# A decoder layer on one core: the sparse tile's output rows, queries and choice go first and on raw weights, and 64 dense tokens instead of 32 take their down products from gathered rows

## The reference

```python
x = x + concat(short_conv(h), hgrn2(h)) @ w_out     # h = rmsnorm(x)
x = x + memory_cross_attention(rmsnorm(x), rmsnorm(mem), wq, wkv, wo)
h = rmsnorm(x)
q = h @ w_query                                     # 8 heads x 2 halves x 128
s = einsum('nhpd,hpkd->nhpk', q, sub_keys)          # 128 keys a half
s_top, i_top = top_k(s, 16)                         # then 16 of the 256 sums: expert_idx, gate
a = gelu(einsum('nd,nhkd->nhk', h, expert_down[expert_idx]))
y = einsum('nhk,nhkd->nd', gate * a, expert_up[expert_idx])
out = rmsnorm(x + y, final_norm_w)
```

## Time and profile before

| | |
|---|---|
| median of 3 runs | 1629.14 us (1626.0 to 1629.47) |
| the profiled execution | 1624.01 us |
| its span, first to last instruction | 1622.3 us |
| granted TensorE clock | 0.999 |
| busy: PE, PEld, DVE, ACT, POOL | 1600.3, 1422.6, 1133.7, 673.2, 829.1 us |
| moved by DMA | 424.69 MB, mean 262 GB/s |

### The profile page before, as it was taken

One profiled execution on the slowest core, in us unless ns is written; L12 is line 12 of the kernel. 1 busy time (PEld: TensorE's weight loads), 2 busy tenths in 40 slices (PEclk: granted clock), 3 DMA queues, 4 the chain that ended last, 5 costly groups with the idle time before them and its releaser, 6 DMA issues.

```text
span 1622.3 us, 26556 instructions
## 1 busy us (share of the span) xinstructions
PE 1600.3 (99%) x9227; PEld 1422.6 (88%) x9227; DVE 1133.7 (70%) x2214; ACT 673.2 (41%) x998; POOL 829.1 (51%) x523
## 2 busy tenths in 40 slices
PE   8999999999999999999999999999999999999998
PEld 6888888788889999999999999998888888888886
DVE  4155451351509999996999898329888888888887
ACT  5342453451534343534545544444333333333333
POOL 4463276423244998987787777866422222222220
PEclk9999999999999999999999999999999999999999
DMA  4322242313434999997999999949999999999992
GB/s 184 93 100 71 75 151 94 104 53 117 146 102 131 347 340 332 329 335 233 339 405 394 387 403 401 362 158 391 400 348 350 331 349 339 349 334 348 339 331 77
DMA packets 154425, 424.69 MB, mean 262 GB/s; under 512 B 15728, under 2 KB 65904, under 8 KB 154224
## 3 DMA queue, kind: packets, MB, share of 16 engines
q1 hardware_dynamic: 89088, 229.41, 40.5%
q0 software_dynamic: 41472, 151.01, 25.5%
q10 hardware_dynamic: 23792, 43.33, 6.9%
HBM read 379.88 MB, written 43.25 MB: 261 GB/s over the span
## 4 chain that ended last, share of the span: by engine, by line
PE 69%; issue 16%; POOL 9%; DVE 2%; DMA 2%; ACT 1%; POOLq 0%; SPq 0%; ACTq 0%; DVEq 0%
PE psum L1471 22%; PE psum L1473 22%; PE psum L1472 22%; POOL w_low L461 8%; PE psum L1766 4%; DMA gate_dram<-arena 1%; DMA kept<-down_in 1%; POOL arena L493 1%; DMA arena<-down_rows,arena 0%; DVE arena L1258 0%; ACT w_high L581 0%; DVE arena L1202 0%; DVE arena L1193 0%; DVE arena L1194 0%; DMA kept<-front_w 0%
## 5 line engine op out<-in xcount | busy, mean ns | idle before, releaser
L461 POOL TENSOR_TENSOR w_low<-kept,w_high 128x1024 fp32r<-128x1024 f32 x212 | 519.5, 2454 | 320.3 <-ACT w_high L581 317.6
L1471 PE MATMUL psum<-hT_high,w_high 128*128 128x352 f32 (+2 forms) x1408 | 484.4, 344 | 7.2 <-POOL w_low L461 5.5
L1473 PE MATMUL psum<-hT_high,w_low 128*128 128x352 f32 (+2 forms) x1408 | 476.6, 339 | 0.0
L1472 PE MATMUL psum<-hT_low,w_high 128*128 128x352 f32 (+2 forms) x1408 | 476.4, 338 | 0.0
L581 ACT ACTIVATE w_high<-kept 128x1024 fp32r<-128x1024 f32 x212 | 224.0, 1058 | 202.6 <-DMA kept<-down_in 102.0
L1471 PE MATMUL psum<-up_high,wgt_high 128*128 128x512 f32 x768 | 298.8, 389 | 0.0
L1473 PE MATMUL psum<-up_high,wgt_low 128*128 128x512 f32 x768 | 298.8, 389 | 0.0
L1472 PE MATMUL psum<-up_low,wgt_high 128*128 128x512 f32 x768 | 298.8, 389 | 0.0
L1471 PEld LDWEIGHTS psum<-hT_high,w_high 128*128 128x128 f32 x1408 | 264.8, 188 | 24.2 <-POOL w_low L461 8.2
L1473 PEld LDWEIGHTS psum<-hT_high,w_low 128*128 128x128 f32 x1408 | 264.7, 188 | 12.7
L1472 PEld LDWEIGHTS psum<-hT_low,w_high 128*128 128x128 f32 x1408 | 264.8, 188 | 12.3 <-issue 0.5
(11 more groups left out here) (252 smaller groups left out, 1956.4 us busy)
## 6 DMA issues: line engine op xcount, KB each, us to landing
kept<-down_in SPq DMA_DIRECT2D x128, 512.0 KB
arena<-up_in SPq DMA_DIRECT2D x128, 512.0 KB, 4.7
kept<-front_w SPq DMA_DIRECT2D x92, 512.0 KB
gate_dram<-arena ACTq DMA_DIRECT2D x40, 512.0 KB
hid_dram<-arena ACTq DMA_DIRECT2D x112, 176.0 KB
arena<-hid_dram SPq DMA_DIRECT2D x112, 176.0 KB
under_w<-gate_dram SPq DMA_DIRECT2D x24, 640.0 KB
arena<-gate_dram SPq DMA_DIRECT2D x8, 640.0 KB
```

What stands on the lines that cost most here:

```text
L461: nc.gpsimd.tensor_tensor(w_low[:, s, :], ring[:, s, :], w_hi[:, s, :].bitcast(F32), ALU.subtract).then_inc(low_ready, 1)
L1471: nc.tensor.matmul(out, lhs[0], rhs[0], start=first, stop=False)
L1472: nc.tensor.matmul(out, lhs[0], rhs[1], start=False, stop=False)
L1473: return nc.tensor.matmul(out, lhs[1], rhs[0], start=False, stop=last)
```

## The change

**Order of the front.** The output product and the queries are split by tile. Tile 3's attention output is kept apart in float32 (`ao_s`), and its output rows are 16 raw matmuls of 512 columns on eight blocks loaded for it alone; then its norm, 12 raw query blocks (queries 0 to 11), the keys of three groups, and later four more raw query blocks. The dense tiles' output product (three tiles) is cut around them: block 60 ahead, block 61 behind the raw rows, the rest behind the keys. No dense query block has tile 3's columns any more. 108 blocks are loaded in the front instead of 92 (`FRONT_ORDER`, `USED`).

**Choice and gathers.** The sparse choice begins after the first key group, in four parts; ahead of its last part VectorE does the dense tiles' residual rows and norm (`dense_rows`). Gathers begin at query block 78, and 18 row products (`EARLY`) are done ahead of the dense choice.

**Edge.** `EDGE` is 64, so `DE` is 320, `EDGE_SLOTS` 64 and `ROWS` 192 instead of 160. `DOTS_A` is 84, G takes 69 row products and E 39. In E, seven low halves are made by VectorE instead of GpSimd (`dve_low`). The edge's gelu, and with it the split of tile 2's gates, moves from gate step 12 and 20 to 23 and 27.

```diff
-RAW0, RAW = 68, 8
-QPOS = RAW0 + RAW
-USED = FRONT + RAW
+FRONT_ORDER = tuple(range(61)) + tuple(range(60, 68)) + (61,) + tuple(range(68, 80)) + tuple(range(62, 68)) \
+    + tuple(range(80, 84)) + tuple(range(68, 84))
+OUT_S, OUT_1, QUERY_S, OUT_2, QUERY_S3, QUERY = 61, 69, 70, 82, 88, 92
+USED = len(FRONT_ORDER)
...
-EDGE = 32
+EDGE = 64
 PARTS = P // EDGE
 EDGE_SLOTS = SLOTS // PARTS
 DE = DN - EDGE
-E0, E_BASE = P - EDGE, P - 32
+E0 = P - EDGE
 ROWS = SLOTS + EDGE_SLOTS
-FIRST_EDGE = 44
-GEL_AT, SPLIT_AT, LAST_TURN = 12, 20, 28
+FIRST_EDGE = 48
+GEL_AT, SPLIT_AT, LAST_TURN = 23, 27, 28
 DOTS_SCORES = (3, 3, 3, 3)
 DOTS_CAND = (1, 1, 1, 1)
 DOTS_HOT = 6
-DOTS_A = DT * (sum(DOTS_SCORES) + sum(DOTS_CAND) + DOTS_HOT)
-DOTS_STEP = (0, 0) + (2,) * 10 + (1, 2, 2) * 12
-DOTS_END = (1,) * 14
+EARLY = 18
+DOTS_A = EARLY + DT * (sum(DOTS_SCORES) + sum(DOTS_CAND) + DOTS_HOT)
+DOTS_STEP = (0, 0) + (1, 2) * 23 + (1,)
+DOTS_END = (3, 2) * 7 + (3, 1)
...
-FIRST_GATHER = 0
+FIRST_GATHER = 78
...
+        def dve_low(i):
+            return DURING <= i < NK - 6 and i % 2 == 1
...
+            for place in range(OUT_S // RING * RING, USED):
+                sp.wait_ge(block_used, place + 1 - RING)
+                load_block(FRONT_ORDER[place], place % RING)
...
-            for i in range(AHEAD + 2):
-                low(FRONT + i, i % 4)
-                if i == FIRST_GATHER:
+            for b in range(76, FRONT + AHEAD + 2):
+                low(b, b % 4)
+                if b == FIRST_GATHER:
                     pool.wait_ge(idx_ready, 1)
...
+                    pool.wait_ge(ffnn.tr, KC)
+                if b < FIRST_GATHER:
+                    goal = 0
+                elif b < FRONT:
+                    goal = 5 + 2 * (b - FIRST_GATHER)
+                elif b < FRONT + 2:
+                    goal = 5 + 2 * (FRONT - 1 - FIRST_GATHER) + 4 * (b - FRONT + 1)
+                else:
+                    first = 5 + 2 * (FRONT - 1 - FIRST_GATHER) + 8
+                    goal = first + (DOTS_A - first) * (b - FRONT - 1) // (AHEAD - 12)
+                while k < min(goal, DOTS_A):
                     down_row(k)
                     k += 1
+            assert k == DOTS_A
...
             for i in range(AHEAD + 2, NK):
-                low(FRONT + i, i % 4)
+                if not dve_low(i):
+                    low(FRONT + i, i % 4)
...
-                    nc.scalar.activation(hT_half[0][:, 2 * h + c, :], psum[:, 6 + c, :], ACT.Copy).then_inc(ao_high, 1)
+                    nc.scalar.activation(ao_s[:, 2 * h + c, :], psum[:, 6 + c, DN:SEQ], ACT.Copy).then_inc(ao_raw, 1)
+                    nc.scalar.activation(hT_half[0][:, 2 * h + c, 0:DN], psum[:, 6 + c, 0:DN], ACT.Copy).then_inc(ao_high, 1)
...
+            for place in range(OUT_2 + 2, QUERY_S3):
+                high_at(place)
+            for t in range(DT):
+                act.wait_ge(x_added_to, MIXED + 2 + DT + t + 1)
+                square(ffnn, t)
+            root(ffnn, 0, DT)
+            high_at(QUERY)
+            sparse_query_out(3)
+            high_at(QUERY + 1)
+            norm_high(ffnn, range(4))
+            sparse_key_out(3)
+            norm_high(ffnn, range(4, KC))
...
+            def dense_rows():
+
+                dve.wait_ge(block_used, OUT_2 + 2)
+                for t in range(DT):
+                    attended_row(t, 0, OB[0][t])
+                for t in range(DT):
+                    if t < DT - 1:
+                        dve.wait_ge(product_done, MIX_PRODUCTS + t + 1)
+                    else:
+                        dve.wait_ge(block_used, OUT_2 + 6)
+                    attended_row(t, 1, OB[1][t])
+                norm_rows(ffnn)
+                norm_gain(ffnn)
...
+            choose(score[:, ST, :], sparse_k, 0, (0, 0, 0, 0), (0, 0, 0, 0), 0, sparse_k.hk, 0, (1, 2, 3, 4), dense_rows)
             nc.vector.scalar_tensor_tensor(idx3.bitcast(U32), sparse_k.hk[:, 0, :], float(NK), sparse_k.hk[:, 1, :],
                                            ALU.mult, ALU.add).then_inc(idx_ready, 1)
-            step(gates_of(sparse_k, gate3, 1))
             dve.wait_ge(ld_last, 32)
-            dve.wait_ge(qp_out, 16)
             step(nc.vector.tensor_tensor(h_row, hn[:, ST, :], ffn_row, ALU.mult))
             step(nc.vector.tensor_copy(own_h, h_chunks))
+            kd = dots(0, EARLY)
+            step(gates_of(sparse_k, gate3, 1))
...
+            for i in range(DURING, DURING + len(DOTS_END)):
+                if dve_low(i):
+                    dve.wait_ge(high_ready, FRONT + i + 1)
+                    nc.vector.tensor_tensor(w_low[:, i % 4, :], ring[:, i % 4, :], w_hi[:, i % 4, :].bitcast(F32),
+                                            ALU.subtract).then_inc(end_low_ready, 1)
+                kd = dots(kd, DOTS_END[i - DURING])
+            assert kd == ROWS
...
+            out_rows(0, 0)
             attend(3)
-            product(hT_half, 60, product_done, ((sc_exp, NT * MH), (ao_out, 2 * MH)), TILES_LAST, ao_out, begun=1)
+            for n in range(8):
+                hf, s, place = n // 4, n % 4, OUT_S + n
+                if n == 4:
+                    pe.wait_ge(pT_out, MT * MH)
+                pe.wait_ge(wt[place % RING], 16 * (place // RING + 1))
+                for j in range(2):
+                    pe.wait_ge(ao_raw, 2 * s + j + 1)
+                    ins = nc.tensor.matmul(psum[:, 4 * hf, :], ao_s[:, 2 * s + j, :], ring[:, place % RING, j * 512:(j + 1) * 512],
+                                           start=(s == 0 and j == 0), stop=(s == 3 and j == 1))
+                ins.then_inc(block_used, 1)
+            out_rows(0, 1)
             pe.wait_ge(ffns.h, 1)
...
+            pe.wait_ge(ao_out, 2 * MH)
+            for g in range(3):
+                sparse_queries(QUERY_S + 4 * g, g)
...
+            for g in range(3):
                 sparse_keys(g)
...
+            out_rows(0, 2)
+            out_rows(0, 3)
+            pe.wait_ge(pk_out, 1)
+            for s in range(4):
+                out_rows(1, s)
+            pe.wait_ge(pk_out, 2)
+            sparse_queries(QUERY_S3, 3)
+            turn_tiles(ffnn)
+            sparse_keys(3)
+            pe.wait_ge(pk_out, 3)
+            pe.wait_ge(low_ready, 69)
...
+                columns(68 + n, n % 4, hT_half, DN, QDB[n % 4])
...
+            for i in range(DURING, NK):
+                if dve_low(i):
+                    pe.wait_ge(end_low_ready, sum(dve_low(j) for j in range(i + 1)))
+                first_product(i, i % 4, FRONT + sum(not dve_low(j) for j in range(i + 1)))
```

247 lines of the change are left out of this document (105 added, 142 removed).

## The result

The changed kernel took 1664.86 us (median of 4 runs, 1656.99 to 1674.01) against 1627.99 (4 runs, 1626.0 to 1629.47): a ratio of 1.0237, interval 1.0212 to 1.0261. The forecast was 1625, its range ended at 1642. It lost 37 us where a gain of 3.6 was worked out.

The account below looks back on a forecast made before the run. TensorE was taken to set the time, with VectorE and GpSimd close behind in A and transfers in G. Front +14.0, A -10.5, G -15.3 and E +8.2 gave -3.6 us, so 1625.5 us, range 1609 to 1642.

Parts of the forecast that it names:

- Front, +16.6 for +14.0: Front, up to down block 0: net work +7.7 us plus waits, less small breaks, forecast +14.0 us.
- A, 244 for 227: Down blocks 0 to 59: 225 us from VectorE and GpSimd plus 2 for ScalarE, 227 against 237.5.
- two bounds side by side: Stage A: VectorE's dense choice gives 225 us, GpSimd's gathers and low halves 224; both bounds say 225.
- its work between is unchanged, 220 us: Stage A: VectorE's dense choice with its row products still takes 220 us, and block 59 follows its last result.
- one for one: Front: if gathers for the 18 early row products come later, VectorE starts the dense choice late by as much.
- G, 244.6 for 239.9: The 48 down blocks with gate steps: narrower matmuls save 15.3 us, to 5.00 us a step.
- Up to 2 us of waiting there are hidden: Stage G, split of the gates moved to step 27, its transfer three steps before: VectorE's lead hides up to 2 us.
- about three steps: Stage G: VectorE leads TensorE by about three gate steps.
- E, 105 for 85: The last 20 down products: block 127 ends at 85 us against 76.8, +8.2 us.
- the 72 us of transfers: Stage E: 28.7 MB at 400 GB/s take 72 us, so the 35th row product falls at 60 of the stage.
- nearer to the saturated one since demand is higher: Stage E: transfer rate taken as 400 GB/s, between 416 in the fastest earlier stretch and 342 with gathers.
- Rival 2: Transfers bind earlier: at 342 GB/s E's bytes take 84 us, kernel 1637.5, at worst 1655; chance 0.20.

Follow-up runs that it names:

- e13: The changed kernel with two of stage A's gathers issued one block later (behind blocks 32 and 39 instead of 31 and 38); 1668.8 us, ratio 1.0268.
- e2: The changed kernel with eight slots instead of four for gathered rows in stage E; 1663.5 us, ratio 1.0214.
- e6: The changed kernel with only the first 11 of 192 gathers issued, all products still done (result not computed); 1597.8 us, ratio 0.9822.
- e1: The changed kernel with each down product waiting for the low half only ahead of its last 8 matmuls; 1657.2 us, ratio 1.0185.
- e11: The changed kernel with the low half waited for last, eight slots in E and the split of the gates later; 1656.0 us, ratio 1.0177.
- e16: The changed kernel with low half waited for last, later gate split, eight slots from E's row product 15, four more gathers behind block 113; 1650.3 us, ratio 1.0140.
- e3: The changed kernel with stage A's 61 gathers spread over 55 blocks instead of 48; 1675.8 us, ratio 1.0287.
- e7: The changed kernel with the edge's gelu at gate step 22 instead of 23 and the split at 29 instead of 27; 1662.8 us, ratio 1.0224.
- e9: The changed kernel with every gather after a slot's first use fetching 8 of 128 rows (result not computed); 1637.3 us, ratio 1.0064.

## Why the prediction was wrong

**What held.** Matmuls of 320 columns start 0.147 us apart. Gate steps are 4.96 us. The second product's 522 us are unchanged. The first three-pass block behind the raw output waited 2.45 us (forecast 3.1), the first dense query block 1.57 (2.1). Five query blocks with two gathers cost 2.7 us of waiting (2.4). TensorE did wait for low halves in E, from block 110 on (forecast 112).

**Front, +16.6 for +14.0.** Of the 2.6 us, 1.7 are the granted clock: behind the waits of 1.33 and 2.45 us it was 0.63 for 4.6 us. Another 0.5 is the border of the earlier trace rows.

**A, 244 for 227, the first step that failed.** The forecast priced GpSimd and VectorE each by itself, found 225 for both, and took them as two bounds side by side. The price of GpSimd's own work, 48 blocks at 3.53 and 13 more gathers at 1.26, was right as far as it goes: TensorE's 211 and 13 gaps of 1.1 to 1.3 us behind double gathers make 227. What was missing is that the two engines stop each other, and that lists so full have no slack for it.

GpSimd waits for VectorE: 10.4 us for slots in A. A single stall of this kind (3.82 us in the timeline below) goes through to TensorE in full, and TensorE comes back at half its clock:

```profile
661.50 0.95 POOL L499 DMA_INDIRECT arena<-down_rows,arena  x1 [0.16 <-issue]
...
666.27 0.94 POOL L499 DMA_INDIRECT arena<-down_rows,arena  x1 [3.82 <-DVE arena L1204]
...
667.23 2.36 POOL L467 TENSOR_TENSOR w_low<-kept,w_high 128x1024 fp32r<-128x1024 f32 x1
...
669.64 0.41 PE L1496 MATMUL psum<-hT_high,w_high 128*128 128x320 f32 x1 [4.46 <-POOL w_low L467]
...
669.89 0.43 PE L1497 MATMUL psum<-hT_low,w_high 128*128 128x320 f32 x1
...
671.18 0.47 PE L1496 MATMUL psum<-hT_high,w_high 128*128 128x320 f32 x1
...
671.45 0.47 PE L1497 MATMUL psum<-hT_low,w_high 128*128 128x320 f32 x1
...
673.62 0.31 PE L1497 MATMUL psum<-hT_low,w_high 128*128 128x320 f32 x1
...
673.77 0.30 PE L1498 MATMUL psum<-hT_high,w_low 128*128 128x320 f32 x1
...
664.90:669.60 4.70, 0.28 (x2) 0.01 (x1) 4.70 (x24) 1.72 (x2) 3.29 (x2) 1.00 0.94 326
...
669.60:673.30 3.70, 3.66 (x14) 3.66 (x15) 3.70 (x11) 0.02 (x1) 3.38 (x3) 0.54 0.73 232
```

Behind 4.46 us of idle time the starts lie 0.267 us apart, which is 320 columns at 1.2 GHz, the lower level, until 673.3; then 0.147 again. The block takes 5.15 us instead of 3.52. Adding up every spacing between 0.2 and 0.4 us inside down blocks, the half clock took 5.8 us in A and 8.5 in E. The account of A: 211 for the matmuls, 26.5 in gaps (16 in a dozen and a half of up to 1.7, most of them behind double gathers, and two of 4.6 and 5.7 behind slot waits), 6 in spacing. e13 shows that the particular stall doesn't matter; others stood in its place.

VectorE waits for GpSimd, and this the forecast left out in "its work between is unchanged, 220 us". Some of its instructions (`TENSOR_TENSOR`, `TENSOR_SCALAR` and `CAST` that read from `arena` or `kept` alone) last longer when they meet a low half on GpSimd: they end only after it. The choice's searches, and the row products, which read `psum` as well, keep their time. One of the first kind in the change, beside the low half that it met, and the same instruction in e2, where it lasted 1.23 us (min/median/max ns):

```profile
638.56 3.97 DVE L1200 TENSOR_TENSOR psum<-arena 128x1024 f32<-128x1024 f32 x1
...
639.01 2.42 POOL L467 TENSOR_TENSOR w_low<-kept,w_high 128x1024 fp32r<-128x1024 f32 x1
...
L1219 DVE TENSOR_TENSOR psum<-arena x1: 1232/1232/1232, 640.8 to 640.8; 128x1024 f32<-128x1024 f32 x1
```

In A of the change fourteen instructions of VectorE were longer than usual in this way, by 29 us together; before nine, by 16.5, and without gathers (e6) five, by 8. The dense choice, from its first instruction to its last, took 228.4 us against 220.1 before and 209.7 in e6, and began 3.8 us into A instead of 1.0, since rows for the early products came late ("one for one", as the forecast had warned) and one such long instruction stood ahead of it. The profile's chain that ended last, followed back as far as it goes, is VectorE for 108 of the 113 us from 635 to 748, up to the gather and the low half of block 50, behind which TensorE has no more than half a microsecond of gaps to the end of A. Its shares of that stretch by line:

```profile
by line: DVE arena L1204 31.3%; DVE arena L1224 10.7%; DVE arena L1215 7.0%; DVE arena L1216 7.0%; DVE arena L1246 6.1%; DVE arena L1220 6.1%; DVE arena L1211 5.2%; DVE arena L1282 3.9%; DVE psum L1200 3.5%; DVE arena L1240 3.1%; DVE psum L
```

So e6's 219 does not clear VectorE. In e1, e11 and e16, which repair the waits for low halves, the choice took 234 to 237 us and ended 1.4 us ahead of block 59: since block 59 needs its last result (0.6 us behind it in e3), A could not have been shorter there by more than a microsecond, whatever was repaired. How the 17 us divide between GpSimd's full list and VectorE's longer choice no run shows; none keeps the gathers and moves these instructions of VectorE out of the low halves' way.

**G, 244.6 for 239.9.** "Up to 2 us of waiting there are hidden" was the step: the way of the edge's values by DMA to the partitions of the gates was taken to be covered, but its two points moved from 8 steps apart (12 and 20) to 4 (23 and 27), and VectorE stood 7.25 us. The lead of "about three steps" was read too high, too: 11.2 us are two steps of 5.3. e7, with 7 steps between the points, gave 5.3 back.

**E, 105 for 85, the second step that failed.** The sum had the product behind which the last low halves stand, the 35th, start 60 us into E; it started at 76.7, and E ended 28 us later, against 25 in the forecast. The term that failed is the 72 us of transfers, in both its factors. DMA over the forecast's own stretch, from 11.2 us before E to that product, of the change and of e16:

```profile
DMA packets 9695, 32.54 MB, mean 371 GB/s; under 512 B 1085, under 2 KB 2072, under 8 KB 9691
...
DMA packets 9762, 32.77 MB, mean 402 GB/s; under 512 B 1092, under 2 KB 2084, under 8 KB 9758
```

The bytes were 32.5 MB and not 28.7: 18.8 of gathered rows (17.3), 10.4 of weights (9.4), 3.4 of stores (2.0). At 400 GB/s that is 10 us more. And the rate was 371 and not 400, "nearer to the saturated one since demand is higher", which is 6 us more. Demand was not higher, since four slots cap it. A gather is 7.2 us on its way, then come issue and product, about 9 us for a turn of four, 2.2 us a product; 39 of them are 86 us, and the last one did start at 86. With eight slots (e16) the same stretch ran at 402 and the 35th product started at 70. So the forecast's 400 is what the transfers can do, and not what four slots ask for. Rival 2 had the rate within E (342; 345 from its start to the last product) for another reason: it took the transfers as the limit, and e16 shows 393 to 410 with eight slots. A late product then frees a slot late, the low half stands behind the gather in the list, and TensorE's clock falls as well.

The forecast's 85 is about what E takes when rows weigh almost nothing (e9, 88.1). What is still open is why the same A takes 238 in one run and 250 in another (the length of the choice varies with it, 220 to 230 us, but not in step), and what the other 4 us on a gather's way are.

## What to carry to other kernels

A list that is filled to its engine's pace by a sum of durations is not at its pace: each wait of one item for another engine goes through in full, and that engine may be waiting for this one. Read from the trace before which of its instructions last longer beside the other's, and leave slack for it. (Moving the waits to an engine whose list nobody stands behind would be another way; it was not tried here.) A ring of n slots fed by gathers gives n products per (way + issue + product), however few the bytes; work that out beside the GB/s before moving products into a stage. And wait for the operand that is late ahead of the first instruction that reads it, not ahead of the group: on the kernel before that alone was worth 0.45%, more than the change was forecast to give; it helps as long as each block is late by less than the cover.

## What was not expected of the hardware

Half the rows a gather: 7.2 us on its way became 6.6, and DMA share stayed at 0.83 in E while GB/s fell from 311 to 230. A high share says that packets are on their way, not that the bytes are at a ceiling. Behind an idle gap of TensorE of only 1.9 us (up to 1037.8, in E) its granted clock was 0.59 over the next 4.2 us, though behind gaps of about 1 us, one every four blocks in A, it stayed at 1.00. And VectorE's 1.2 us instruction took 4 us beside a low half on GpSimd, while searches and row products there kept their time.
